# Six more input pieces of the first mixer in high and low parts, the low parts made by GpSimd

## The reference, cut to what matters

```
p = h @ w_in
a_val, a_gate, q, k, v, r, glr = split(p)
y_a = silu(layer_norm(depthwise_conv_31(a_val * sigmoid(a_gate))))
log_a = log_sigmoid(glr @ gate_w2 + gate_b) / 16
o   = gated linear attention of q, k, v with decays exp(cumsum(log_a))
y_b = rms_norm(o) * silu(r)
x   = x + concat(y_a, y_b) @ w_out
```

## Time and profile before

| what | value |
|---|---|
| median of three runs | 2264.03 us (2264.0 to 2265.94) |
| profiled execution, device time | 2263.34 us |
| its span | 2261.6 us |
| TensorE / VectorE / ScalarE / GpSimd busy | 98% / 70% / 53% / 38% |
| granted TensorE clock, mean | 0.998 |
| first mixer's projection and attention | about the first 110 us of the span |

### The profile page before, as it was taken

How to read it: one execution, slowest core, us unless ns; L and a number is a source line. 1 busy time by engine, 2 the same in 40 slices (tenths; PEclk the granted TensorE clock), 3 DMA queues, 4 the chain that set the end, 5 groups by cost and what they waited for, 6 DMA issues and landing times.

```text
span 2261.6 us, 43986 instructions
## 1 busy us (share of the span) xinstructions
PE 2219.5 (98%) x14360; PEld 1936.9 (86%) x14360; DVE 1578.5 (70%) x3193; ACT 1209.9 (53%) x1908; POOL 858.6 (38%) x777
## 2 busy tenths in 40 slices
PE   8999999999999999998999999999999999999999
PEld 7889888888888888897998888888888888888877
DVE  5744885888888755545268768888886555655885
ACT  5255556555444455556465565554444456555764
POOL 1067887333344100033778853323440003743000
PEclk9999999999999999999999999999999999999999
DMA  5345656555555666553556655555555665444655
GB/s 160 103 138 161 187 187 184 175 169 172 179 170 175 185 191 191 179 185 99 169 160 188 190 179 168 176 168 177 176 176 186 195 192 173 149 140 142 188 174 165
DMA packets 109651, 385.65 MB, mean 171 GB/s; under 512 B 12512, under 2 KB 14848, under 8 KB 109312
## 3 DMA queue, kind: packets, MB, share of 16 engines
q1 hardware_dynamic: 106864, 382.34, 54.5%
q10 hardware_dynamic: 2704, 2.23, 0.3%
HBM read 383.46 MB, written 1.06 MB: 170 GB/s over the span
## 4 chain that ended last, share of the span: by engine, by line
PE 93%; DVE 3%; ACT 2%; issue 1%; DMA 0%; POOL 0%; SPq 0%; DVEq 0%; ACTq 0%
PE bank L2134 23%; PE bank L2114 12%; PE bank L2184 11%; PE bank L2186 11%; PE bank L2185 11%; PE bank L2031 3%; PE bank L2035 3%; PE bank L2043 3%; PE bank L2449 3%; PE bank L2241 2%; PE bank L2417 1%; DVE x_parts L1162 1%; PE bank L2235 1%; PE bank L2071 1%; PE bank L2078 1%
## 5 line engine op out<-in xcount | busy, mean ns | idle before, releaser
L538 ACT ACTIVATE w_hi<-ring 128x1024 fp32r<-128x1024 f32 x697 | 735.9, 1057 | 533.9 <-PE bank L2186 395.0
L412 POOL TENSOR_TENSOR w_lo<-ring,w_hi 128x1024 fp32r<-128x1024 f32 x229 | 552.2, 2418 | 724.4 <-ACT w_hi L538 709.4
L1121 DVE TENSOR_TENSOR w_lo<-ring,w_hi 128x1024 fp32r<-128x1024 f32 x468 | 572.7, 1224 | 225.6 <-ACT w_hi L538 225.6
L2134 PE MATMUL bank<-x_parts,w_hi 128*128 128x512 f32 x2320 | 583.5, 393 | 0.2 <-ACT w_hi L538 0.2
L2134 PEld LDWEIGHTS bank<-x_parts,w_hi 128*128 128x128 f32 x2320 | 416.9, 189 | 75.4 <-issue 0.4
L2184 PE MATMUL bank<-w_hi,x_parts 128*128 128x512 f32 x1112 | 435.5, 392 | 0.9 <-DVE x_parts L1128 0.9
L2186 PE MATMUL bank<-w_lo,x_parts 128*128 128x512 f32 x1112 | 432.8, 389 | 0.0
L2185 PE MATMUL bank<-w_hi,x_parts 128*128 128x512 f32 x1112 | 432.6, 389 | 0.0
L424 POOL COPY quads<-sco 128x32 f16 (+1 forms) x256 | 218.8, 882 | 459.7 <-DVE sco L1579 459.6
L2114 PEld LDWEIGHTS bank<-x_parts,w_lo 128*128 128x128 f32 x2368 | 324.8, 190 | 24.8 <-DVE w_lo L1121 2.9
L2114 PE MATMUL bank<-x_parts,w_lo 128*128 128x256 f32 x2368 | 336.8, 283 | 0.2 <-DVE w_lo L1121 0.2
(11 more groups left out here) (317 smaller groups left out, 2472.7 us busy)
## 6 DMA issues: line engine op xcount, KB each, us to landing
ring<-u_dram SPq DMA_DIRECT2D x256, 512.0 KB, 3.6
ring<-v_dram SPq DMA_DIRECT2D x256, 512.0 KB, 3.5
ring<-up_dram SPq DMA_DIRECT2D x44, 512.0 KB, 3.8
ring<-wq_dram SPq DMA_DIRECT2D x32, 512.0 KB, 3.5
ring<-sb_in_dram SPq DMA_DIRECT2D x31, 512.0 KB, 3.5
ring<-od_in_dram SPq DMA_DIRECT2D x25, 512.0 KB, 3.7
ring<-down_dram SPq DMA_DIRECT2D x22, 512.0 KB, 3.5
ring<-ev_in_dram SPq DMA_DIRECT2D x21, 512.0 KB, 3.5
```

The source lines that it names most:

```text
L412: pool.tensor_tensor(w_lo[:, k % RING, :], ring[:, k % RING, :], w_hi[:, k % RING, :].bitcast(F32), ALU.subtract).then_inc(g["lo_pool"], 1)
L538: A(w_hi[:, k % RING, :], ring[:, k % RING, :], ACT.Copy).then_inc(g["w_hi_done"], 1)
L1121: V.tensor_tensor(w_lo[:, k % RING, :], ring[:, k % RING, :], w_hi[:, k % RING, :].bitcast(F32), ALU.subtract).then_inc(g["lo_dve"], 1)
L2134: mm(dst[:, :], hi[:, rows[c]], x_both[:, c, :], start=(c == 0), stop=False, skip_group_check=True)
```

## The change

Pieces 7 to 12, that is the second gate unit, q and k, are used in high and low parts, as 19 and 20 were. GpSimd makes their lows. ScalarE makes their highs at seven calls of `highs` that are put between its other instructions (one piece each, for pieces 7 to 12). The wait for the activations' lows moves to the head of unit 4.

```diff
-EV_WHOLE = 19
+EV_SPLIT = (7, 13, 19)
...
-        RUNS = [("ev_in", "ev_in", EV_WHOLE, WHOLE), ("ev_in_b", "ev_in", 21 - EV_WHOLE, POOL),
+        RUNS = [("ev_in", "ev_in", EV_SPLIT[0], WHOLE), ("ev_in_b", "ev_in", EV_SPLIT[1] - EV_SPLIT[0], POOL),
+                ("ev_in_c", "ev_in", EV_SPLIT[2] - EV_SPLIT[1], WHOLE), ("ev_in_d", "ev_in", 21 - EV_SPLIT[2], POOL),
...
-                if name == "ev_in_b":
+                if name == "ev_in_d":
...
-            for k in range(EV_WHOLE, 21):
-                low(starts["ev_in"] + k)
+            for k in (*range(EV_SPLIT[0], EV_SPLIT[1]), *range(EV_SPLIT[2], 21)):
+                low(k)
...
                 A(xh[:, 2 * j:2 * j + 2, :], b3(xg[:, j * 512:(j + 1) * 512], 2), ACT.Copy).then_inc(g["ev_x_hi"], 1)
+            highs(8)
             act.wait_ge(g["ev_z_in"], 2)
...
             gate(0)
+            highs(9)
             nc.scalar.preload_act_table(ACT.Exp)
...
                 A(e_dif[lv], e_dif[lv], ACT.Exp).then_inc(g["ev_difexp"], 1)
+                if lv == 2:
+                    highs(10)
             act.wait_ge(g["ev_fade"], 1)
             A(e_kd, e_kd, ACT.Exp).then_inc(g["ev_expk"], 1)
+            highs(11)
             nc.scalar.preload_act_table(ACT.Sigmoid)
+            highs(12)
             gate(1)
+            highs(13)
...
-            for _ in range(4):
-                whole_unit()
+            whole_unit()
+            pe.wait_ge(g["ev_x_lo"], 4)
+            for _ in range(3):
+                one_unit(features)
             whole_unit(by_token=True)
...
             pe.wait_ge(g["units_out"], 8)
-            pe.wait_ge(g["ev_x_lo"], 4)
```

## The result

| | before | after |
|---|---|---|
| median of 10 executions each, same chip, us | 2264.81 (2261.46 to 2269.86) | 2270.26 (2269.34 to 2271.97) |
| profiled execution, us | 2263.34 | 2269.43 |
| its span, us | 2261.6 | 2267.7 |
| span, root's turn to outputs, us | 66.90 | 72.31 |

The changed kernel is slower: ratio 1.0023, 95% interval 1.0016 to 1.0031, a difference of 5.45 us where the forecast was +8.0 (median 2272.0, range 2267 to 2276). Direction and range hold; the size was 2.5 us too large.

The account below looks back on a forecast made before the run. The stage was taken as bound by TensorE with VectorE some 8 us behind. The terms 2.9 + 10.7 - 1.67 - 6.06 + 2.1 gave +8.0 us, added to the median: 2272.0 us, range 2267 to 2276.

Parts of the forecast that it names:

- TensorE's saving: On TensorE, six pieces used in parts instead of whole save 0.574 us each, 3.44 us.
- ScalarE and the hold of low 7: At VectorE's first decay instruction: piece 7's high delays ScalarE's Abs, its low then holds VectorE; 2.9 us together.
- Five holds until k: In VectorE's list before its reading of k: lows of pieces 8 to 12 each hold it 2.14 us, 10.7 us.
- second rival: Before k, holds fall partly into idle time or GpSimd waits: half the holds, +2.5, up to +4.5 us; 15%.
- Who releases level 0: At level 0's start on TensorE: it waits for VectorE's k, done at 69.7, with unit 7 ending near 68.
- TensorE's gaps for the highs of pieces 9 and 12: On TensorE before k: waits of about 1 us for piece 9's high and about 54.3 to 57.8 for piece 12's.
- Idle time given back: In VectorE's list from k to the last `take`: all 6.06 us of idle time disappear.
- gaps of VectorE after 60: Sign in the profile after: if VectorE shows gaps after 60 us, its slack was not used up.
- 5.9: At VectorE's last `take`: starting from k at 69.7 without idle, it comes at 94.85, +5.9 us.
- The second hold at the end, +2.1: Before the states: the low of piece 20 also holds a tap of VectorE, +2.1 us; either 0 or 2.1.
- The clock, 0 with a bound of 1.7: After TensorE's gap before the outputs: loss at half clock taken as 0, with +1.7 us as upper bound.
- third rival: Clock falls after the outputs' gap, or waits on TensorE delay a level too: +9.7 to +12 us; 18%.

Follow-up runs that it names:

- e1: The changed kernel with GpSimd's lows of pieces 7 to 12 over 8 columns instead of 1024; median 2259.05 us.
- e2: The changed kernel with the high of piece 7 moved behind ScalarE's Abs, Exp and Ln; median 2271.43 us.
- e6: The kernel before with only pieces 11 and 12 (k) also used in parts, lows by GpSimd; ratio 0.9990 against the kernel before.
- e7: The kernel before with only pieces 5 and 6 (unit 3) also used in parts, lows by GpSimd; ratio 0.9996 against the kernel before.
- e8: The kernel before with pieces 5, 6, 11 and 12 also used in parts, lows by GpSimd; ratio 0.9999 against the kernel before.
- e4: The kernel before plus six low-sized subtractions by GpSimd that nobody waits for, no piece changed; median 2267.79 us.
- e3: The changed kernel with the high of piece 12 made before the second sigmoid; median 2269.45 us.

## Why the prediction was right, and where its size was off

Point by point, counted from the turn of the root:

- **TensorE's saving.** 3.44 us forecast. e1 has 3.08 in the stage and 3.8 ± 0.8 at equal clock. Right.
- **ScalarE and the hold of low 7.** 2.9 forecast, 2.32 for the start of the decay and 0.34 for its hold: 2.66. Right in size, but e1 shows that the delay costs nothing alone, and e2 that removing it calls up a full hold. It was a price only because the holds had used up the slack.
- **Five holds until k.** 10.7 forecast; from the rows 38.42, 45.58, 47.24, 49.65 and 60.13, each less its usual 0.42, 0.41, 0.41, 0.47 and 0.47, it is 2.21 + 1.34 + 2.08 + 2.15 + 1.52 = 9.30. The mechanism is right. The size is off where GpSimd had to wait for the port: lows 9 and 12 took 3.76 and 4.50 us, of which the first 1.5 and 2.2 cost VectorE nothing. My second rival said this of half of them; it held for two of five. k is 10.1 us late, 11.9 was forecast.
- **Who releases level 0.** The prediction had it wait for k (69.7), with unit 7 done near 68. In after unit 7 was the later one: from the turn it ended at 40.3 us, against 38.9 for k. TensorE's gaps for the highs of pieces 9 and 12 came much as forecast (about 1 and 3.5 us; found 0.77 and 3.11). That for the high of piece 10 (1.3) didn't; in its place stand two that the prediction lacked, 1.60 us for the low of piece 9 and 1.16 us for that of piece 12, the two that had been shut out of the port. So the holds act by two ways, through VectorE's own list and through the high and the low of piece 12 that TensorE waits for, and the second way ended last.
- **Idle time given back.** 6.06 forecast, 4.53 found (1.53 is left: VectorE waits for TensorE at 80.31, 93.94 and 95.04). The prediction had named this sign of being wrong itself, gaps of VectorE after 60. By VectorE's list alone the last `take` would have moved by 10.1 - 6.06 = 4.0 us; TensorE's lateness made it 95.04 - 88.96 - 0.66 = 5.4. That 5.9 was forecast is near by luck: VectorE's path was put too long by 1.9 us, and TensorE's, which decided, too short by 1.3.
- **The second hold at the end, +2.1.** This step failed: the prediction took 2.1 "because VectorE waits for nobody at that point whereas before it waited for TensorE". VectorE still waited for TensorE, 0.41 us before the last `take`, as before, so tap and low met exactly as in the earlier trace rows: one tap of 2.58, and the second low beside PSUM readers. The term is 0. With 5.4 instead of 5.9 it explains the stage: 8.0 - 2.1 - 0.5 = 5.4. The wait of some 2.5 us that the prediction saw before the outputs is 0.39 for the same reason.
- **The clock, 0 with a bound of 1.7.** Two stretches at half clock came up to unit 10. The first lies in the stage, hidden behind the wait for the low of piece 12; the second, behind the outputs, cost 1.5 us in the profiled execution. Over the timed executions: after's mean clock is 0.9969, that of the kernel before here 0.9974 to 0.9979. With 1.74 us for 0.001 this is 0.9 to 1.7 us, and 4.1 + 1.3 gives the 5.4 measured. So the third rival's fall of the clock did occur behind the outputs, at about its price, though without the gap that the prediction had put before it. It made up for part of the term of 2.1 that failed: the total of +8.0 against +5.4 is nearer than its parts.

By the Trainium skill (SBUF — State Buffer, "SBUF: two separate sides") whoever starts first has the port pair for the whole instruction. The prediction weighed a full 2.60 us for each hold by it. The runs agree on the blocking and show less for its cost: where the low comes in at once, VectorE loses about the low's length less the usual length of the held instruction (2.57 - 0.42 at 38.42, 2.21 lost). The page is silent on who wins when instructions of VectorE follow each other without a gap. Here GpSimd came in right behind the instruction under way (held are 38.42, 47.24, 49.65 and 97.45), or only when VectorE had gone over to a PSUM reading (44.97, 59.52), and what decides between the two stays open.

## What to carry to other kernels

GpSimd working on SBUF is no free helper beside a VectorE that works on SBUF: five subtractions by GpSimd, 2.4 to 2.6 us long where they came in at once, cost VectorE 1.3 to 2.2 us each, and it would have needed 1.2 for the same work. Count VectorE's slack up to the next result that somebody waits for, and compare it with the holds: one fits here (e6, e7), as do three (e8), and six don't (e4). Look also at who waits for GpSimd's own result, since GpSimd can be kept out as well. Lows belong where VectorE reads PSUM or waits, and a change that gives VectorE an earlier start can lose that cover again.

## What was not expected of the hardware

- A TENSOR_SCALAR with one tensor input from SBUF was held as well: 1.75 and 2.49 us instead of 0.41 at 45.58 and 47.24, and 2.66 instead of 0.43 in e7. I had counted only instructions with both inputs in SBUF.
- GpSimd can be shut out through a run of VectorE instructions: a subtraction of 8 columns took 1.48 us instead of 0.20 (e1), one of 1024 columns 4.50 instead of 2.4.
- Half-clock stretches come at different places in kernels that differ little, one of them with 0.39 us of idle time near it. Inside the stage they cost about 1.5 us in e3 and e4, more than the 1.2 us that two pieces bring. A difference of 0.001 in the mean granted clock goes with 1.74 us of span here, so that changes of 1 or 2 us are hard to see unless the clock is taken out.
